# Which engine makes the low weight parts of twenty weight pieces in each layer of the second kind

## The reference, cut to what matters

```python
h = rms_norm_2(x, g_mix_norm)
proj = h @ w_in
m_qk, m_v, m_o, m_i, m_f, moba_qkv, cq, ckv, kpe = jnp.split(proj, offsets, axis=-1)
qk = jax.nn.silu(causal_depthwise_conv(m_qk, conv_w, conv_b))          # gated queries and keys
...                                                                      # gated recurrence -> hm
aq, ak, av = jnp.split(moba_qkv.reshape(B, S, 3 * MOBA_HEADS, MOBA_DH), 3, axis=2)
aq, ak = rms_norm_2(aq, g_moba_q), rms_norm_2(ak, g_moba_k)              # then partly rotated
ha = rms_norm_2(moba_attention(aq, ak, av), g_moba_out)                  # block branch
lq = (rms_norm_2(cq, g_cq) @ w_uq).reshape(B, S, MLA_HEADS, MLA_QK_DIM)  # latent branch
kv = (rms_norm_2(ckv, g_ckv) @ w_ukv).reshape(B, S, MLA_HEADS, MLA_NOPE + MLA_DV)
...                                                                      # -> hl
x = x + mix @ w_out
x = x + jnp.square(jax.nn.relu(rms_norm_2(x, g_mlp_norm) @ w_up)) @ w_down
```

## Time and profile before

| what | value |
|---|---|
| median of three runs (lowest, highest) | 2012.46 us (2009.29, 2016.42) |
| profiled execution: span from first to last instruction | 2010.0 us |
| profiled execution: time with what lies around the span | not recorded apart |
| granted TensorE clock, mean over the span | 0.962 of full |
| PE / VectorE / ScalarE / GpSimd busy | 1878.0 / 1288.2 / 1093.3 / 916.6 us |
| the two layers of the second kind | from about 1245 us and 1622 us of the span to its end |

### The profile page before, as it was taken

The page is one execution under the profiler, slowest core; times in us unless marked ns, Lnnn a source line. Parts: engine busy times, 40 slices in busy tenths (PEclk is TensorE's granted clock), DMA queues, the critical chain, the costliest instruction groups (busy, mean ns, idle before and its releaser), DMA issues.

```text
span 2010.0 us, 43300 instructions
## 1 busy us (share of the span) xinstructions
PE 1878.0 (93%) x15850; PEld 1747.4 (87%) x15850; DVE 1288.2 (64%) x1956; ACT 1093.3 (54%) x1862; POOL 916.6 (46%) x662
## 2 busy tenths in 40 slices
PE   9898889999999898889999989998899999989999
PEld 8878778999999878778999988866899997669999
DVE  4587725679924487825679963576786536777754
ACT  5653455557755643455557755665555547465543
POOL 4543449929986543449919985721100024220000
PEclk9999889999999999989999999997999999879999
DMA  6432015656665432005656655420466653215665
GB/s 213 134 111 66 11 38 158 178 159 184 188 182 175 140 109 72 23 30 153 176 159 182 186 164 156 143 89 21 135 185 200 186 168 108 76 31 166 188 187 165
DMA packets 146916, 271.12 MB, mean 135 GB/s; under 512 B 16433, under 2 KB 16946, under 8 KB 146738
## 3 DMA queue, kind: packets, MB, share of 16 engines
q1 hardware_dynamic: 145296, 264.97, 44.5%
q10 hardware_dynamic: 1442, 3.66, 0.5%
HBM read 267.52 MB, written 1.05 MB: 134 GB/s over the span
## 4 chain that ended last, share of the span: by engine, by line
PE 57%; DVE 21%; POOL 11%; ACT 8%; issue 3%; DMA 0%; ACTq 0%; DVEq 0%; SPq 0%
PE bank L668 56%; POOL ring_split L1360 11%; ACT arena L1394 6%; DVE arena L2468 4%; DVE hidden_lo L1949 3%; DVE hidden_hi L1948 2%; DVE arena L2474 2%; PE bank L810 1%; ACT hi_ring L1394 1%; DVE u_split L2035 1%; DVE u L2030 1%; DVE arena L2558 0%; DVE arena L2190 0%; DVE small L2284 0%; DVE arena L2282 0%
## 5 line engine op out<-in xcount | busy, mean ns | idle before, releaser
L1360 POOL TENSOR_TENSOR ring_split<-ring,hi_ring 128x512 fp32r<-128x512 f32 x602 | 847.7, 1436 | 798.4 <-ACT hi_ring L1394 795.1
L1394 ACT ACTIVATE hi_ring<-ring 128x512 fp32r<-128x512 f32 x890 | 549.6, 630 | 524.1 <-PE bank L668 479.5
L668 PE MATMUL bank<-u_hi,hi_ring 128*128 128x256 f32 (+1 forms) x2160 | 617.9, 286 | 31.4 <-POOL ring_split L1360 30.6
L668 PE MATMUL bank<-u_split,hi_ring 128*128 128x256 f32 (+1 forms) x2160 | 605.5, 280 | 0.0
L668 PE MATMUL bank<-u_hi,ring_split 128*128 128x256 f32 (+1 forms) x2160 | 605.4, 280 | 0.0
L668 PEld LDWEIGHTS bank<-u_hi,hi_ring 128*128 128x128 f32 (+1 forms) x2160 | 404.7, 187 | 44.2 <-POOL ring_split L1360 31.5
L668 PEld LDWEIGHTS bank<-u_split,hi_ring 128*128 128x128 f32 (+1 forms) x2160 | 404.5, 187 | 1.7
L668 PEld LDWEIGHTS bank<-u_hi,ring_split 128*128 128x128 f32 (+1 forms) x2160 | 405.1, 188 | 1.0
L2074 DVE TENSOR_TENSOR ring_split<-ring,hi_ring 128x512 fp32r<-128x512 f32 x288 | 194.1, 695 | 114.1 <-ACT hi_ring L1394 111.0
L668 PE MATMUL bank<-hidden_hi,hi_ring 128*128 128x256 f32 x864 | 244.7, 283 | 13.4 <-POOL ring_split L1360 13.3
L668 PEld LDWEIGHTS bank<-arena 64*64 64x64 f32 (+3 forms) x3680 | 211.8, 156 | 50.9 <-issue 31.2
(11 more groups left out here) (265 smaller groups left out, 2502.3 us busy)
## 6 DMA issues: line engine op xcount, KB each, us to landing
ring<-in_stream SPq DMA_DIRECT2D x1002, 256.0 KB, 2.6
par<-in_params ACTq DMA_DIRECT2D x3, 637.0 KB, 3.9
h<-in_x SPq DMA_DIRECT2D x4, 256.0 KB, 4.0
cst<-in_cst SPq DMA_DIRECT2D x1, 993.0 KB
out<-h ACTq DMA_DIRECT2D x3, 256.0 KB, 2.7
par<-in_params ACTq DMA_DIRECT2D x1, 633.0 KB, 6.5
out<-h ACTq DMA_DIRECT2D x2, 128.0 KB, 2.2
msk<-in_masks SPq DMA_DIRECT2D x1, 104.0 KB
```

What stands on the lines that cost most here:

```text
L668: ins = nc.tensor.matmul(o, l, r, start=start, stop=stop)
L1360: G.tensor_tensor(ring_lo[:, c, :], ring[:, c, :], hi_ring[:, s % HI_RING, :].bitcast(F32), ALU.subtract).then_inc(lo_by_pool, 1)
L1394: return nc.scalar.activation(o, i, f, **kw)
```

## The change

Five names join `BY_VECTOR2`: the four pieces each of `aq`, `ak`, `av`, `qk0` and `qk1` get their low parts from VectorE, 20 in a layer, 40 in all. Four calls put them into VectorE's program, each with lead 0. GpSimd's program loses the same 40 instructions. PE's and ScalarE's instructions and their order stay; PE's waits for these pieces are for VectorE's counter now.

```diff
-BY_VECTOR2 = {"WO", "D"} | {f"U{i}" for i in range(2, 16)}
+BY_VECTOR2 = {"aq", "ak", "av", "qk0", "qk1", "WO", "D"} | {f"U{i}" for i in range(2, 16)}
...
                 norm_parts(C, p("g_mix"), rn[:] if l else roots["gained"][0], 0, layers[0] * PIECES1 + l * PIECES2, None if l else final_scale)
+                lo.upto("aq", 0)
                 factor = gained_scale if l == 0 else rn[:]
...
+                lo.upto("av", 0)
                 refine(C, "latents", 1)
...
                 split(C, cqk, cqk_hi, cqk_lo, S["latents_ready"])
 
+                lo.upto("qk0", 0)
                 refine(C, "block qk", 2)
+                lo.upto("qk1", 0)
                 for i, n in ((0, "g_mq"), (2, "g_mk")):
```

## The result

The changed kernel took 2020.4 us (median of 20 runs, 2013.7 to 2025.7), the kernel before 2012.9 us beside it (20 runs). The ratio is 1.0044, 95% interval 1.0032 to 1.0057: slower by 8.9 us, with 6.4 to 11.5 us as the interval. (The ratio is made from all the runs and not from the two medians, which lie 7.5 us apart.) Forecast were 8.4 us and 2021 us.

A forecast was written before the change was run, and what follows sets the result against it. PE was taken to set the pace, with GpSimd entering where PE waits for low parts. (2.8 + 1.4) x 2 = 8.4 us on 2012.5 gave 2020.9, say 2021 us; range 2013 to 2029, the forecast's own 2017 to 2026.

The forecast's parts named there:

- `aq`, `ak` at nothing, `av` 0.6 us won: Later latents' scaling is covered by PE's aq and ak pieces; PE's wait in av's last piece shrinks by 0.6 us.
- The chain at 6.4 us, because GpSimd is idle: VectorE's latents' root, gains and split, ahead of qk0's low parts, take 6.4 us undisturbed, in place of 11.26.
- PE idle 5.5 us at `qk0`: PE waits 5.5 us per layer for qk0's first low part behind VectorE's latents' work, where it had no wait.
- `qk1`'s wait of 1.85 us and 1.4 us for the clock: New 1.85 us PE wait at qk1 behind the block branch's root; lower clock over qk0 adds up to 1.4 us a layer.
- `uq` 2.8 us later and 1.4 for the clock: Per layer, uq starts 2.8 us later than before, plus 1.4 us from PE's lower clock after the idle time.
- All of it reaches the end: From uq on, later stages follow PE's products in a chain, so the whole delay of 8.4 us reaches the end.
- Rival 1: Faster: VectorE's cheaper low parts reach qk0 in time and the GpSimd waits vanish, 8.5 us won, 2004 us; chance 0.07.
- the convolution waits for `qk1` anyway: VectorE's convolution waits for PE's qk1 in any case; given beside the claim that the whole delay is passed on.
- Rival 2: No change: waits moved equal those removed, or a later wait shrinks; some 1.5 us a layer left, 2015 us; chance 0.20.
- Rival 3: Much slower: VectorE's long instructions have another cause than GpSimd and stay long, 2034 us; chance 0.08.

The follow-up runs named there:

- the constants: The changed kernel with four added GpSimd subtractions of 128x512 constants into unread memory beside VectorE's latents' chain: ratio 1.0086, 2026.4 us.
- the clock held: The changed kernel with eleven added PE matmuls of constants into qk0's bank ahead of its first piece: ratio 1.0033, 2016.2 us.
- the control with freed banks: The kernel before, with ScalarE copying raw qk0 and qk1 and freeing their banks, the convolution reading the copy, its second half behind the rotations: ratio 1.0007.

## Why the prediction was right, step by step

- *`aq`, `ak` at nothing, `av` 0.6 us won.* Right. The wait in `av` fell by 0.68 and 0.54 us, and the experiment with these alone lost nothing.
- *The chain at 6.4 us, because GpSimd is idle.* Right at 6.41, and its cause is shown: 6.4 where GpSimd was idle beside it for another reason (only `qk0` moved), 9.4 and 10.0 where it worked (`qk0` left to it, and the constants). The rule of the Trainium skill that the prediction weighed (GPSIMD Engine Reference, 8. Key points) is borne out by these runs.
- *PE idle 5.5 us at `qk0`.* 5.30 and 5.38.
- *`qk1`'s wait of 1.85 us and 1.4 us for the clock.* Their sum, 3.25 us, came out as 3.55 and 3.56 us: `qk0`'s start to `qk1`'s took 9.29 and 9.30 us, against 5.74 in both layers before. How the two share it differs, since a slower `qk0` eats the wait (0.78 us in the first layer). With the clock held, the wait alone is 2.22 and 2.06, a little over the 1.85.
- *`uq` 2.8 us later and 1.4 for the clock.* A little too small: 24 to 26 us were given from `av` to `uq`, and it took 26.07 and 27.56. In the second layer the granted clock fell once more behind `qk1`'s wait of 2.05 us (0.76 over 1685.2 to 1692.4 us), and `qk1` took 7.26 us in place of 5.73. The sum has no term for that.
- *All of it reaches the end.* Not quite: of the 4.75 and 6.2 us by which `uq` is later, net of the shift at the layer's start, 3.90 and 4.15 are left behind the attention. Why is not settled. One part may be chance: from `uq` to that place the granted clock was 0.88 in the trace before and 0.89 in that after in the first layer, 0.83 and 0.88 in the second. GpSimd's waits there fell too, from 3.2 to 0.5 us in the first layer, while others grew. The two misses, `uq` too late and not all of it passed on, offset each other; that 8.05 us in the profile and 8.9 in the runs stand so near to 8.4 is so far luck.
- *Rival 1, the cheaper low part wins,* was priced at 2004 us for the case that the chain is out of the way. It was refuted for this change. Putting the low parts first wasn't enough, though, as rival 1 assumed: 2015 us. The prediction's sentence that the convolution waits for `qk1` anyway holds for the change, in which VectorE waits 4.75 us for PE behind the convolution (1.10 before); it fails with the low parts in the order of need, where PE waits for the banks that the convolution frees. With the banks freed early the kernel took 2002 us.
- *Rival 2, the idle time is made up,* was priced at 2015 us. At most a small part of it came true: of 10.95 us at `uq` in both layers 8.05 are left behind the attention, and the ratio of no change, 1, lies outside the measured interval.
- *Rival 3* needs VectorE to stay slow; it took GpSimd at work beside it to come near it, 2026 us.

## What to carry to other kernels

A cheaper instruction on a faster engine gains only if its place in that engine's program is ahead of the need: look at what stands in front of it and what that waits for, before its price. Then look at what stands behind it, down to buffers that the engine frees late, because the next bound there shows only when the first is gone. Where two engines slow each other, moving work off one of them can shorten what stays on the other: here VectorE's chain went from 11.26 to 6.41 us as GpSimd fell idle beside it.

## What the runs showed of the hardware that was not expected

**TensorE's step at full clock had two values.** At a granted clock of 1.00, matmuls of the same shape in the last down product were 172 in 20 us in the profile before and 179 in that after. From one start to the next it was 0.118 and 0.113 us.

```profile
1940.00:1960.00 20.00, 20.00 (x172) 20.00 (x171) 9.84 (x15) 9.06 (x15) 0.00 (x0) 1.00 0.65 191
```

```profile
1950.00:1970.00 20.00, 20.00 (x179) 20.00 (x178) 10.65 (x16) 9.35 (x15) 0.00 (x0) 1.00 0.65 193
```

From 1924.97 to 2005.06 us before the work is that from 1933.65 to 2010.72 after: 80.1 and 77.1 us, a difference of 3.0 us far behind the low parts that moved. The step doesn't go with the engine that makes the low parts: over 1940 to 1960 us the control with freed banks, whose low parts are GpSimd's, had 179 matmuls, and so had the kernel with all but `qk0` moved; the kernels with only `qk0` moved and with PE kept at work had 173 and 172. It may be a part of the 10 us over which the runs of one kernel scatter; that, and what sets the step, stays open. Hence a difference of two profiled spans says little here; differences between places within one stage, and ratios over many runs, say more.

**Where VectorE's inputs lay decided whether GpSimd slowed it.** In the kernel before, the convolution with one input in a bank took 3.07 us for six instructions beside a busy GpSimd:

```profile
1302.79 3.07 DVE L2536 SCALAR_TENSOR_TENSOR arena<-bank,par,arena 128x255 f32<-128x255 f32 x6 [0.22 <-DVE small L2526]
```

```profile
1295.53 12.91 POOL L1360 TENSOR_TENSOR ring_split<-ring,hi_ring 128x512 fp32r<-128x512 f32 x8
```

With both inputs in the arena, in the control with freed banks, six took 7.24 us beside the same low parts, which GpSimd made from 1299.07 to 1312.69:

```profile
1306.25 7.24 DVE L2543 SCALAR_TENSOR_TENSOR arena<-arena,par 128x255 f32<-128x255 f32 x6
```

and 3.08 us with GpSimd idle (with freed banks and the low parts in the order of need, from 1310.69). The Trainium skill says that a VectorE instruction with at most one SBUF input, outside the 2-port modes, doesn't contend with GpSimd, and that one with two contends with a GpSimd instruction that reads SBUF (SBUF — State Buffer, Who interferes with whom). The rows agree with both halves, 3.07 us for the first and 7.24 against 3.08 for the second.
